# Two reorderings around the expert loop of a two-layer encoder: when result rows are gathered, and where VectorE splits an inner row

## The reference

```python
logits = (xf @ w_router) + b_router            # 256 x 8
top_v, top_e = lax.top_k(logits, 2)            # two experts for each token
gate = jax.nn.softmax(top_v, axis=-1)
# for each expert e and its tokens:
y = (silu(h @ wg[e]) * (h @ wu[e])) @ wd[e]    # 1024 -> 3584 -> 1024, 8 experts
out[token] += gate * y                         # both experts of a token are summed
```

## Time and profile before

| | |
|---|---|
| median of 3 runs | 1973.07 us (1972.71 to 1978.49) |
| profiled execution | 1969.99 us |
| its span, first to last instruction | 1968.1 us |
| PE busy | 1882.6 us, 96% of the span |
| DVE busy | 1411.7 us, 72% |
| ACT busy | 1154.5 us, 59% |
| POOL busy | 76.5 us, 4% |
| DMA | 527.40 MB, mean 268 GB/s |
| mean granted clock of TensorE | 0.985 |
| matmuls, and weight loads ahead of them | 9632 each |

### The profile page before, as it was taken

The page is one execution under the profiler, slowest core; times in us unless marked ns, Lnnn a source line. Parts: engine busy times, 40 slices in busy tenths (PEclk is TensorE's granted clock), DMA queues, the critical chain, the costliest instruction groups (busy, mean ns, idle before and its releaser), DMA issues.

```text
span 1968.1 us, 26070 instructions
## 1 busy us (share of the span) xinstructions
PE 1882.6 (96%) x9632; PEld 1542.2 (78%) x9632; DVE 1411.7 (72%) x1453; ACT 1154.5 (59%) x1129; POOL 76.5 (4%) x130
## 2 busy tenths in 40 slices
PE   6899999999998899999999999999999999999996
PEld 5787677999996787676788787888888888888775
DVE  3578564555546557665688888888888888888885
ACT  3455553333325456554677777777777777777662
POOL 2101002000001100001000000000000000000100
PEclk9999999999999999998999999999999999999997
DMA  9547546555545634344899999999999999999990
GB/s 296 163 142 236 169 156 214 183 177 180 178 137 215 193 119 138 110 149 177 303 371 364 380 365 376 375 361 387 365 383 373 366 378 364 387 369 373 389 336 23
DMA packets 242816, 527.40 MB, mean 268 GB/s; under 512 B 9040, under 2 KB 58352, under 8 KB 242624
## 3 DMA queue, kind: packets, MB, share of 16 engines
q1 hardware_dynamic: 234272, 497.65, 71.2%
q0 software_dynamic: 6320, 21.02, 3.2%
q10 hardware_dynamic: 2160, 7.87, 1.0%
HBM read 510.78 MB, written 15.73 MB: 268 GB/s over the span
## 4 chain that ended last, share of the span: by engine, by line
PE 86%; DVE 5%; DMA 3%; ACT 3%; issue 2%; SPq 0%; POOL 0%; ACTq 0%; POOLq 0%; DVEq 0%
PE ps L1255 28%; PE ps L1198 19%; PE ps L1157 9%; PE ps L1054 9%; PE ps L1042 4%; PE ps L1381 4%; PE ps L1020 3%; PE ps L1073 3%; DMA ring<-in_moe_w_down_dram 2%; PE ps L1132 1%; PE ps L1425 1%; PE ps L1227 1%; ACT down_hi_w L1671 1%; PE ps L1342 1%; DVE ring_lo L2009 1%
## 5 line engine op out<-in xcount | busy, mean ns | idle before, releaser
L2220 DVE TENSOR_TENSOR ring_lo<-ring,up_gate_hi_w 128x2048 fp32r<-128x2048 f32 x224 | 506.9, 2289 | 74.0 <-ACT up_gate_hi_w L1668 73.2
L1668 ACT CAST up_gate_hi_w<-ring 128x2048 fp32r<-128x2048 f32 x224 | 425.2, 1915 | 102.4 <-DMA ring<-in_moe_w_gate_dram 85.0
L1255 PE MATMUL ps<-up_gate_hi_w,tokens_hi 128*128 128x512 f32 x896 | 354.5, 396 | 4.4 <-DVE tokens_lo L2243 2.8
L1255 PE MATMUL ps<-up_gate_hi_w,tokens_lo 128*128 128x512 f32 x896 | 349.5, 390 | 0.0
L1255 PE MATMUL ps<-ring_lo,tokens_hi 128*128 128x512 f32 x896 | 349.0, 389 | 0.0
L1671 ACT CAST down_hi_w<-ring 128x2048 fp32r<-128x2048 f32 x112 | 213.7, 1913 | 70.6 <-DMA ring<-in_moe_w_down_dram 64.6
L2225 DVE TENSOR_TENSOR down_lo_w<-ring,down_hi_w 128x2048 fp32r<-128x2048 f32 x112 | 252.3, 2286 | 3.1 <-ACT down_hi_w L1671 3.1
L1255 PEld LDWEIGHTS ps<-up_gate_hi_w,tokens_hi 128*128 128x128 f32 x896 | 168.3, 188 | 39.9 <-DVE tokens_lo L2243 4.7
L1255 PEld LDWEIGHTS ps<-up_gate_hi_w,tokens_lo 128*128 128x128 f32 x896 | 168.2, 188 | 35.9
L1255 PEld LDWEIGHTS ps<-ring_lo,tokens_hi 128*128 128x128 f32 x896 | 168.4, 188 | 33.5
L1198 PE MATMUL ps<-down_hi_w,hidden_hi 128*128 128x512 f32 x576 | 184.2, 401 | 8.0 <-DVE hidden_lo L2236 6.8
(11 more groups left out here) (268 smaller groups left out, 3045.3 us busy)
## 6 DMA issues: line engine op xcount, KB each, us to landing
ring<-in_moe_w_gate_dram SPq DMA_DIRECT2D x112, 1024.0 KB, 5.2
ring<-in_moe_w_up_dram SPq DMA_DIRECT2D x112, 1024.0 KB, 5.2
ring<-in_moe_w_down_dram SPq DMA_DIRECT2D x112, 1024.0 KB, 8.8
ring<-in_w_in_dram SPq DMA_DIRECT2D x58, 1024.0 KB, 5.4
ring<-in_ffn_w_up_dram SPq DMA_DIRECT2D x16, 1024.0 KB, 5.3
ring<-in_ffn_w_gate_dram SPq DMA_DIRECT2D x16, 1024.0 KB, 7.9
ring<-in_ffn_w_down_dram SPq DMA_DIRECT2D x16, 1024.0 KB, 9.6
expert_slot_rows<-work POOLq DMA_DIRECT2D x17, 512.0 KB, 4.9
```

The source lines that it names most:

```text
L1255: m = mm(bank, xs[:, 4 * half + k, :], w[:, k, :], start=(half == k == n == 0), stop=(half == 1 and k == 3 and n == 2))
L1668: copy(up_gate_hi_w[:, j, :], ring[:, slot, :]).then_inc(run.up_gate_hi, 1)
L2220: v.tensor_tensor(ring_lo[:, slot, :], ring[:, slot, :], up_gate_hi_w[:, j, :], ALU.subtract)\
```

## The change

Two things, both in layer 1. POOL waits for one more semaphore before the four gathers: the last cast of a gate or up tile. And DVE's order within a chunk is changed: with `c == 0` the low part of the second half of the tokens stands ahead of the low part of tile 4, and in every chunk the low part of the turned inner row stands between those of tiles 4 and 5. The function is used for the main pass and for the overflow pass, which is not taken with these inputs.

```diff
@@ -964,6 +964,7 @@
                     pool.wait_ge(main_pass.y_stored, 16 * (N_EXPERTS - 1))
                     pool.wait_ge(main_pass.rows_in, 16 * N_EXPERTS)
+                    pool.wait_ge(main_pass.up_gate_hi, 4 * ALL_CHUNKS)
                     for t in range(NT):
                         for n in range(2):
                             nc.gpsimd.indirect_dma_start((second_rows if n else fsum)[:, t, :], None, slot_rows,
@@ -2345,12 +2346,12 @@
                         token_los(run, e, 0)
                     if not no_chunk_before:
                         expert_hidden(run, b - 1)
-                        expert_los(run, b - 1, 4)
                     if c == 0:
                         token_los(run, e, 1)
                     if not no_chunk_before:
+                        expert_los(run, b - 1, 4)
+                        turned_los(run, b - 1)
                         expert_los(run, b - 1, 5)
-                        turned_los(run, b - 1)
                     if not split_before:
                         expert_los(run, b, 2)
                         expert_los(run, b, 3)
```

## The result

| | before | after |
|---|---|---|
| median of the timed runs | 1972.89 us (1971.29 to 1978.49) | 1949.65 us (1947.06 to 1950.6) |
| profiled execution | 1969.99 us | 1947.06 us |
| its span | 1968.1 us | 1945.2 us |
| mean granted clock | 0.985 | 0.985 |

The ratio is 0.9887, with a 95% interval of 0.9873 to 0.9902: 23 us faster by the medians, 22.9 by the spans. Later rounds timed the same kernel at 1951.58 (0.9891) and 1949.23 us (0.9889). The forecast was 1953, the range 1947 to 1964.

The account below looks back on a forecast made before the run. PE bounds the loop, DMA some 6% behind. Gains 9.9 + 2.8 + 4.1 + 3.9 = 20.7, less 1, so 20 us: profiled 1969.99 becomes 1950; with the median 3 us higher, forecast 1953, range 1947 to 1964.

Parts of the forecast that it names:

- What bounds the kernel: In the expert loop PE sets the pace, busy for all of a 17.0 us chunk, with DMA some 6% behind.
- The inner row's low part: Moved ahead of the second down split on DVE, it ends PE's waits at the down product: 9.9 and 2.8 us.
- 0.21 in each of 47 chunks: PE's loss going from gate to down product, waiting for the inner row's low part; removing it gains 9.9 us.
- The sentence on DVE's new wait: In each chunk DVE waits some 0.9 us for the inner row's cast, covered by spare time behind it.
- The long waits: Three long PE waits for the inner row's low part, at late down weights or the loop's start: 2.8 us gained.
- the 1 us taken off for late loads: Deduction for all experts together: chunks with the result's store and token rows need more DMA than the 395 GB/s seen.
- the 9.9: Gain in us at the step onto the down product: 47 chunks at 0.21 us each.
- the rival that the rule stood behind: At the down product, the 0.21 us is the price of any wait ahead of a weight load: 1963, chance 0.11.
- The tokens' low part: Second half moved ahead of the first down split, for 7 experts: PE's token waits of 0.6 us go, 4.1 us.
- The gathers in the loop: Four gathers leave a saturated stretch of the loop, where they lengthened two chunks by 2.91 and 0.95: 3.9 us gained.
- The gathers in the tail: After the last up cast, rows land by 1915.5, before the second tile's use at 1916.4: 0 us, bounds 0 and 4.
- The rival that named this place: In the tail gathers collide, and the rows or ple weights come up to 4 us late: 1957, chance 0.07.

Follow-up runs that it names:

- two-and-two kernel: Against the kernel after, the first two of the four gathers issued one chunk sooner, the other two left; 1946.97 us, ratio 0.9869; repeated 1948.28 us, ratio 0.989.
- third profile: The kernel after, unaltered, run once more in the same rounds as the two-and-two kernel's repeat; 1949.23 us, ratio 0.9889.
- tokens-only kernel: Against the kernel before, only the low part of the tokens' second half moved ahead of the first down split; 1980.95 us, ratio 1.0039.
- spread kernel: Against the kernel after, the four gathers issued one at a time, one in each of the last four chunks; 1952.32 us, ratio 0.989.

## Why the prediction was right, and where it was not

**What bounds the kernel** held: PE busy through every chunk, 16.81 us between multiplications where 16.82 was worked out.

**The inner row's low part.** 0.21 in each of 47 chunks held where it can be read cleanly: the chunks with c = 4 and 5 gained 3.4 in 14, or 0.24 each, and the step onto the down product is 0.227. The sentence on DVE's new wait held too: predicted 0.9, measured 0.89, with 1.25 us between the row's end and its use where 1.2 was worked out; the second split is not waited for. The long waits were worth less than their 2.8: the first eight periods gave 2.1 where 3.9 was reckoned, as another stall of late loads took the place of the one at the start. Against that the chunks with c = 1, 2 and 3 gained 6.6 instead of 3.6: the 1 us taken off for late loads was not lost there, and they gained 0.39 each on average, and not 0.21. One pair with late loads, the second expert's c = 2 and 3, gave 1.75 of the 6.6 (35.07 before, 33.32 after), and the five with c = 1 gave 0.38 each (17.18 to 17.20 before, 16.81 or 16.82 after). It comes with the row's place alone (6.3 in that kernel). What makes the chunks with c = 1 some 0.16 longer than 17.03 in the kernel before I had not looked at, and did not take apart.

Here the Trainium skill's rule ("TensorE: Matmul & The Clock Gate", Part 3: Packing small matmuls) disagrees with the measurement: by it 128-row weight loads overlap no matmul, and the 9.9 would not be there. The step fell to 0.227 us in the trace, with one load ahead of every matmul, and the rival that the rule stood behind was shown wrong. The same section of the Trainium skill also says that a load into the background weight buffer is pulled ahead of running matmuls; the 0.227 would fit that sentence, though no run here tests it by itself, and the prediction had used only the other.

**The tokens' low part.** Its 4.1 us are a term that holds only in company: 4.1 in the six periods (1.1 and 5.6 by the medians of two pairs) with the row's new place, -7.6 without it. The prediction treated its parts as a sum. That is the step that was wrong in kind, though not in this total: it had named the down product as the next user of the split, and not that the row, last in DVE's old order, would be late by the 0.69 that moved ahead of it. With the row's new place beside it that does no harm, so the sum stayed right.

**The gathers in the loop.** 3.9 was right, in the old order (3.9) and in the new one (4.0).

**The gathers in the tail.** Here the forecast was wrong: "the rows are there by 1915.5", 0.9 ahead of their need, and 0 for the tail. In the kernel after, ACT waited 3.48. The same clock, read from the last up cast: the first gather starts 1.77 us after the cast's end and not at once; the last is issued 7.83 and not 6.79 after the first; its rows are used 10.0 and not 8.6 after it. That is 1.8 + 1.0 + 1.4 = 4.2 late, less the 0.9 in hand, 3.3. Of it 12.75 - 10.90 = 1.85 reached `last_y_lo` (1898.17 - 1885.42, and 10.90 before), and 1.5 the end. The rival that named this place had 4 us for it. The prediction's bounds, 0 and 4 us, held it; the value taken was too low. Four ple loads of 1 MB share DMA with the rows, and a mean share of 0.64 over 21 us does not tell that it was 0.91 from 1905.8 to 1912.6 and nothing after 1915.3. The 1.4 does not come from the gathers' move alone: with the old orders the rows were used 8.7 after the last issue. In the kernel after, ACT's last down cast waits 1.00 for its load, and with the gathers alone it does not wait for DMA at all; so loads run later there, which would fit, but no run took it apart. In the two-and-two kernel the last gather is issued 3.4 us after the last up cast (1880.16 to 1883.59), and not 9.6, and nobody waits.

**The total** came out 3.4 us above the truth by the medians. The gain was put 2.4 us too low in the loop and 1.5 too high in the tail, 2.2 us of spread ahead of the loop came on top, and the rest lies in the medians. So the mechanism was right for the row and for the gathers in the loop, and the closeness of the total is in part luck: two terms were off in opposite directions, and the terms of the loop itself missed by 1.8 less at the start and 3.0 more with c = 1, 2 and 3.

## What to carry to other kernels

Read the step of a matmul where PE passes from one product to the next: a step of 0.33 where 0.23 is normal, on an engine that shows 100% busy, was 0.21 us in every chunk, and the fix was the order on another engine. An item of 0.69 that is needed first should not stand behind a split of 2.29 that is needed 2.7 us later: whenever that split's load is late, both are. But it should stand only as far forward as its own input allows: one place further, behind a wait of 3.1 us, it cost 1.1 us in every chunk. Price the parts of a reordering together: one that is worth 4 us beside another cost 7.6 by itself. When a burst is moved out of a saturated loop, ask when the first user in the new place needs it, and try to move half.

## What the runs showed of the hardware

**TensorE's clock falls at different places in the same program.** Windows of 2.75 us from the start of the last down product, first of the kernel after, then of its third profile. Ahead of them PE had done the same, a wait of 0.84 and one of 1.40:

```profile
1888.17:1890.92 2.75, 2.70 (x12) 2.24 (x13) 1.65 (x1) 2.75 (x2) 0.00 (x0) 1.00 1.02 419
```

```profile
1889.35:1892.10 2.75, 2.69 (x7) 2.10 (x8) 1.64 (x2) 2.75 (x2) 0.00 (x0) 0.55 1.02 420
```

At a granted clock of 0.55 (nearly the level of 1.2 GHz) seven matmuls begin where there are twelve at 1.00, and the down product ends 1.6 us later behind the last multiplication (10.14 against 8.55). The third profile's tail is longer by only 0.4 in all (60.2 against 59.8). So differences of a us or two in the tail between single traces are partly this, those of the two-and-two kernel (57.3 and 57.5) among them; both of its traces, and the one with all four gathers sooner, had the low clock in the same place as the third profile, so nothing of their gain is owed to a better clock there. Further on it is: behind `last_y_lo` three products of PE (L1305, the first eight of L1032 and 24 of L1043) take 1.69 + 1.63 + 7.69 = 11.0 us in the two-and-two kernel's chain and 1.54 + 1.98 + 7.70 = 11.2 in its repeat, where they take 12.1, 12.0 and 12.4 in the three traces of the kernel after; through the first of them (L1305) the granted clock was 0.64 and 0.72, and 0.50 in all three traces of the kernel after. That is the 1 us of their shorter tail which does not come from the rows. The tokens-only kernel has a short part behind `last_y_lo` as well, 46.2 us, with the gathers where they were.

**The first indirect DMA after a long pause starts late.** Its start comes 1.77 us after the end of the cast it waits for, in the kernel after (1875.95 to 1877.72), in its repeats (1876.69 to 1878.47, 1877.11 to 1878.88) and with the gathers alone (1896.53 to 1898.30). In the two-and-two kernel the third gather, 12.4 us after the second, starts 0.26 after its cast (1880.16 to 1880.42). What fills the 1.77 the profile does not say. In the spread kernel the second gather comes 14.3 us after the first and starts at once too; whether it is the long pause or being the first of the four that costs, no run tells apart.
